# Expert weights laid out for 8 KB runs, with a stepped read in the gate and up products

## The chip, the core and the metric

The kernel runs on one core of a Trainium2 chip. The metric is the device time of one execution in microseconds (us), the median of the runs shown. Smaller is better. "PE" is TensorE's matmul side, "PEld" its weight loads, "ACT" ScalarE, "DVE" VectorE, "POOL" GpSimd, "SP" SyncE, which issues most of the DMAs.

## What is computed

One layer of a streaming encoder over 576 rows (512 prompt, 64 sample) of width 1024: an input projection, two kinds of attention, an output projection, and then a mixture of experts. The change touches the experts alone:

```
scores = sigmoid(h @ w_router)                  # top 6 of 64 experts per row, within 4 of 8 groups
g = einsum('td,edf->tef', h, w_gate)            # w_gate: 64 experts x 1024 x 256
u = einsum('td,edf->tef', h, w_up)              # w_up:   64 experts x 1024 x 256
a = silu(g) * u * comb[..., None]               # comb: the routing weight, 0 where not chosen
routed = einsum('tef,efd->td', a, w_down)       # w_down: 64 experts x 256 x 1024
shared = (silu(h @ w_sg) * (h @ w_su)) @ w_sd
x = x + g2 * (routed + shared); y = rms(x) * g_final
```

Everything is float32. An expert has 3 matrices of 1 MB (1.049 million bytes) each.

## The kernel before

The program is written engine by engine, with semaphores by hand; the order on each engine is the order of the code. It has three stages. Up to about 567 us come the projections, attention, the router and the sorting of rows to experts. From 567 to 1211 us runs the expert loop. From 1211 us the routed rows are summed and the shared expert and the last norm follow.

**Items.** The 576 x 6 = 3,456 pairs of row and expert are cut into items of at most 64 rows of one expert (`SLOT = 64`), and every expert has at least one. With the inputs used here the routing gives, expert by expert, 1 2 1 1 3 2 2 2 1 1 1 1 2 1 1 1 1 1 1 2 1 1 2 1 1 2 1 1 1 2 3 1 2 2 2 1 1 3 1 2 1 1 1 2 1 1 1 1 1 1 2 1 2 3 1 1 1 1 2 1 1 1 2 1 items, 90 in all. `START` holds the first item of each expert.

**One item.** GpSimd gathers the item's rows of `h_rows` (the normed rows, stored to memory by ACT, L1165 to L1171) into `HG[x]` (`gather`, L508), two half rows of 512 columns per row: partition 64h+s holds half h of row s. ACT copies them to `HGS` (L1186), PE transposes four 128-column blocks (`turn_in`, L917), and DVE copies the result to `HGT`, so that block k of the contraction (k from 0 to 7) is `HGT[:, k % 4, k // 4, :]`. `gate_up` (L920 to L925) makes 16 float32 products: for each k, and for n = 0 and 1, a 64-column stationary block of `HGT` against 256 moving columns, 128 of gate and 128 of up. n picks the half of the 256 expert columns and the half of the array (output partitions n*64). In the trace each float32 product is 2 records, so an item has 32 records of L924. Then follow the transposes of the next item (L917), the down products of the item before (`down`, L931, 8 records), and the transpose of this item's activations (L946). ACT does the silu (L1195), DVE the product with up (L1586), ACT copies the transposed activations to `AE` (L1198), DVE copies the down result to `YO[x]` (L1580, L1588), and GpSimd scatters it to `y_rows` (L516).

**Weights.** There are four buffers for gate and up (`GU[j]`) and four for down (`DN[j]`); expert e uses j = e mod 4. PE waits for all three loads of an expert at once, before its first item (`exp_ld[j]`, 48). SP issues the loads in one queue. `load_wide` (L333 to L335) brings gate and up, `load_down` (L337, L338) brings down. `refill(e, ...)` waits until the last gate/up product of expert e is done and then issues `load_wide(e + 4)`; it then waits until the down products in the first item of expert e are done and issues `load_down(e + 3)`. The first four experts are loaded ahead, gate and up at 502.6 us, down at 535.8 us, once all of `h_rows` is stored.

In these loads partition p takes rows k*128+p of gate and up, which is 8 runs of 1 KB in memory and 8 separate pieces of 1 KB in the buffer (gate and up alternate there), and rows f*128+p of down, which is 2 runs of 4 KB.

Of the kernel before, what the change touches and what calls it, by code (L numbers as in the profile page):

```python
# [19 lines left out]
P = 128  # L20
D = 1024
KC = D // P
# [11 lines left out]
FE = 256  # L34
# [11 lines left out]
def build(nc, x_prompt, x_sample, cache_a_k, cache_a_v, cache_b_k, cache_b_v, c_prompt, c_sample, w_ada, b_ada,  # L46
# [3 lines left out]
    with ctx:  # L50
# [5 lines left out]
        bank = [ctx.enter_context(nc.psum_tensor(f"bank{i}", [P, 512], F32)) for i in range(8)]  # L56
        top = [0]

        def take(n):
            top[0] += n  # L60
            assert top[0] <= N_ARENA, top[0]
            return top[0] - n

        def at(base, *shape, dt=F32):
            n = 1
            for s in shape:
                n *= s
            v = arena[:, base:base + n]
            if dt != F32:
                v = v.bitcast(dt)  # L70
            if len(shape) == 2:
                v = v.rearrange("p (a b) -> p a b", b=shape[1])
            elif len(shape) == 3:
                v = v.rearrange("p (a b c) -> p a b c", b=shape[1], c=shape[2])
            return v
# [3 lines left out]
        a_ring = take(3 * 4096)  # L79
        a_att = take(KC * T * 2 + KC * PAST + NT * D + PT * D)  # L80
# [26 lines left out]
        H2S = at(a_tmp, NT, D)  # L107
        SA = at(a_tmp + 2048, 2, T)

        GU = [RING[0], RING[1], RING[2], at(a_att, KC, 512)]  # L110
        DN = [at(a_att + 4096 + 2048 * i, 2, D) for i in (3, 0, 1, 2)]
        WSG, WSD = GU[0], DN[0]

        HG = [at(a_tmp + 512 * i, 512) for i in range(2)]
# [124 lines left out]
        lt_done, lt_evac, logit_done, sc_ready, h2t_done, h2_evac = map(sem, ("lt_done", "lt_evac", "logit_done", "sc_ready", "h2t_done", "h2_evac"))  # L239
# [4 lines left out]
        exp_ld = [sem(f"exp_ld{i}") for i in range(4)]  # L244
# [62 lines left out]
        def _(sp):  # L307
# [23 lines left out]
                for view, a, b in parts:  # L331
                    sp.dma_start(RING[g % 3][:, :, a:b], view).then_inc(ring_ld[g % 3], 16)
            def load_wide(e, j):  # L333
                sp.dma_start(GU[j][:, :, 0:FE], w_gate[0, bass.ds(e, 1)].rearrange("e (k p) n -> p (e k) n", p=P)).then_inc(exp_ld[j], 16)
                sp.dma_start(GU[j][:, :, FE:2 * FE], w_up[0, bass.ds(e, 1)].rearrange("e (k p) n -> p (e k) n", p=P)).then_inc(exp_ld[j], 16)  # L335

            def load_down(e, j):  # L337
                sp.dma_start(DN[j], w_down[0, bass.ds(e, 1)].rearrange("e (f p) n -> p (e f) n", p=P)).then_inc(exp_ld[j], 16)  # L338


            sp.wait_ge(wo_done, NT)
            for j in range(4):
                load_wide(j, j)
            sp.wait_ge(tr_done, 27)
            sp.wait_ge(h2_stored, 16 * NT)
            for j in range(4):
                load_down(j, j)
            sp.wait_ge(start_ready, 1)

            def refill(e, j, down):  # L350

                first = sp.value_load(START[0:1, bass.ds(e + 1, 1)], min_val=1, max_val=NI)
                sp.wait_ge(gu_done, first)
                load_wide(e + 4, j)
                if down:
                    first = sp.value_load(START[0:1, bass.ds(e, 1)], min_val=1, max_val=NI)
                    sp.wait_ge(dn_done, first + 1)
                    load_down(e + 3, (j + 3) % 4)
# [6 lines left out]
            first = sp.value_load(START[0:1, NE - 4:NE - 3], min_val=1, max_val=NI)  # L365
            sp.wait_ge(dn_done, first + 1)
            load_down(NE - 1, 3)

            first = sp.value_load(START[0:1, NE - 3:NE - 2], min_val=1, max_val=NI)
# [9 lines left out]
            for t in range(NT):  # L379
# [4 lines left out]
                r = ROWS[t]  # L384
                rows = y_rows[t * P * YK:(t * P + r) * YK, :].rearrange("(p k) d -> p k d", k=YK)
                for k, part in YB[t]:
                    sp.dma_start(part[0:r], rows[:, k:k + part.shape[1], :]).then_inc(yb_ld[t], 16)
            for t in range(NT):
                sp.wait_ge(y_ready, t + 1)
                r = ROWS[t]  # L390
# [168 lines left out]
        def _(pe):  # L559
# [92 lines left out]
            for n in range(6):  # L652
                g = G_IN + n
                pe.wait_ge(ring_ld[g % 3], ring_count(g))
                w = RING[g % 3]
# [4 lines left out]
                for t in range(NT if n % 3 == 2 else 4):  # L660
# [9 lines left out]
                    else:  # L670
                        pe.wait_ge(before, base + (3 if t < 2 else 5))
                        r = ROWS[t]
                        for k in range(KC):
                            if t < 4:
                                last = pe.matmul(bank[t][:, :], HT[:, k, t * P:t * P + P], w[:, k, :], start=(k == 0), stop=(k == KC - 1))  # L675
                            else:

                                for x in range(2):
                                    last = pe.matmul(bank[4][x * TS:x * TS + TS, 0:256], HT[:, k, TP:T], w[:, k, 256 * x:256 * x + 256],
                                                     start=(k == 0), stop=(k == KC - 1))  # L680
# [7 lines left out]
            for j in range(PT):  # L688
                for a in range(2):
                    q = 2 * NT + 2 * j + a  # L690
                    pe.wait_ge(kb_evac, q - 1)
                    b = bank[5 + 2 * (q % 2)]
# [161 lines left out]
            w = [RING[(G_OUT + n) % 3] for n in range(2)]  # L854
# [31 lines left out]
            for t in range(NT):  # L886
                if t >= 2:
                    pe.wait_ge(h2_evac, t - 1)
                r = ROWS[t]
# [8 lines left out]
            for u in range(NT * TOPK):  # L898
                t, k = divmod(u, TOPK)
# [19 lines left out]

            def gate_up(j):  # L920
                for k in range(KC):
                    w = GU[j][:, k, :].rearrange("p (g f) -> p g f", f=FE)
                    for n in range(2):
                        last = pe.matmul(bank[0][n * SLOT:n * SLOT + SLOT, 0:2 * P].rearrange("p (g f) -> p g f", f=P), HGT[:, k % 4, k // 4, :],  # L924
                                         w[:, :, n * P:n * P + P], start=(k == 0), stop=(k == KC - 1))  # L925
                last.then_inc(gu_done, 1)

            def down(j):
                for f in range(2):
                    for n in range(2):  # L930
                        last = pe.matmul(bank[3][n * SLOT:n * SLOT + SLOT, :], AE[:, f, :], DN[j][:, f, 512 * n:512 * n + 512], start=(f == 0), stop=(f == 1))  # L931
                last.then_inc(dn_done, 1)

            def item(i, j, before):

                pe.wait_ge(hgt_ready, i + 1)
                gate_up(j)
                pe.wait_ge(hg_staged, i + 2)
                pe.sem_inc(pe_mark)
                turn_in()  # L940
                pe.wait_ge(ae_ready, i + 1)
                pe.wait_ge(yo_ready, i + 1)
                down(before)
                pe.wait_ge(ac_ready, i + 1)
                pe.sem_inc(pe_mark)
                pe.transpose(bank[2][:, 0:P], AC, IDENT).then_inc(at_done, 1)  # L946
# [5 lines left out]
            with pe.Fori(0, NE // 4) as g:  # L952
                e = g * 4
# [21 lines left out]
            for t in range(NT):  # L975
                if t == 4:
                    pe.wait_ge(acc_ready, 1)
                r = ROWS[t]
# [7 lines left out]
        def _(act):  # L986
            n = [0]
# [176 lines left out]
            for t in range(NT):  # L1164
                r = ROWS[t]  # L1165
                b = 6 if t % 2 == 0 else 0
                act.wait_ge(h2t_done, t + 1)
                act.copy(H2S[0:r, t, 0:512], bank[b][0:r, :])
                act.copy(H2S[0:r, t, 512:D], bank[b + 1][0:r, :]).then_inc(h2_evac, 1)
                act.wait_ge(h2_evac, t + 1)  # L1170
                act.dma_start(h2_rows[t * P:t * P + r, :], H2S[0:r, t, :]).then_inc(h2_stored, 16)  # L1171
            for s in range(2):
# [18 lines left out]
            with act.Fori(0, pairs) as g:  # L1191
                for x in range(2):
                    i = g * 2 + x
# [494 lines left out]
```

## Time and profile before

| | |
|---|---|
| time, median of 3 runs | 1307.94 us (1305.64 to 1310.03) |
| span of the profiled execution, first to last instruction | 1303.8 us |
| the profiled execution's own time | its span is what the profile gives; the median run is 4.1 us above that span |
| PE busy | 1130.0 us, 87% |
| ACT, DVE, POOL busy | 324.9, 391.3, 306.5 us |
| DMA | 304.18 MB in 195,436 packets, mean 233 GB/s |
| the expert stage, 567 to 1211 us | PE busy 590.2 of 644 us, DMA engines busy 0.99, 342 GB/s |

Busy shares are averages over stages with different limits, so the stage is read by itself. "PEclk" is the clock that TensorE was granted (1.0 is 2.4 GHz, 0.5 is 1.2 GHz). A DMA share near or above 1 means that the 16 DMA engines had packets all the time. A wait for several loads is put down to the one that came last.

### The profile page before, as it was taken

To read this page: it belongs to the slowest core of one execution; us is meant where nothing else is said; L and a number is where in the kernel's file an instruction comes from. 1 tells how busy PE (TensorE), PEld (TensorE's weight loads), DVE (VectorE), ACT (ScalarE), POOL (GpSimd) and SP (SyncE) were. 2 spreads that over 40 slices of the span, in tenths; PEclk is the share of its full clock that TensorE was granted. 3 is DMA by queue.
4 is the path that set the end of the run, shared out by engine and by line. 5 is a ranking of instruction groups with operands and counts; after the bars stand their busy time and mean duration, and the time that the engine had idled before them with its cause. 6 is when DMAs were issued, how large, how long until landed. Compare 5 with 4: busy or idle time off the path is not lost.

```text
span 1303.8 us, 19553 instructions
## 1 busy us (share of the span) xinstructions
PE 1130.0 (87%) x6570; PEld 656.3 (50%) x6571; DVE 391.3 (30%) x936; ACT 324.9 (25%) x708; POOL 306.5 (24%) x500
## 2 busy tenths in 40 slices
PE   3899999898999897489998698899999889988960
PEld 1676676465666544354554344455554445544630
DVE  2200000284553223622222122222222212222587
ACT  2000100295663111222222222222222212222111
POOL 1000100102222000333333233333333323333123
PEclk9699999998997898689999999999999989999995
DMA  9711321213440005729899999999999999899651
GB/s 320 278 65 65 109 93 65 74 64 130 165 159 1 1 1 186 274 88 351 310 350 372 369 374 369 369 366 314 322 340 363 369 362 371 310 368 329 258 188 72
DMA packets 195436, 304.18 MB, mean 233 GB/s; under 512 B 13206, under 2 KB 146392, under 8 KB 194568
## 3 DMA queue, kind: packets, MB, share of 16 engines
q1 hardware_dynamic: 178488, 268.26, 59.6%
q0 software_dynamic: 16256, 33.08, 7.0%
q10 hardware_dynamic: 656, 2.36, 0.5%
q8 instruction: 23, 0.38, 0.1%
q14 instruction: 13, 0.11, 0.0%
HBM read 290.26 MB, written 33.82 MB: 249 GB/s over the span
## 4 chain that ended last, share of the span: by engine, by line
PE 68%; DMA 12%; DVE 7%; SPq 7%; issue 2%; ACT 2%; POOL 1%; POOLq 0%; DVEq 0%; ACTq 0%
PE bank L924 19%; DMA arena<-in_w_down 10%; PE bank L931 9%; PE bank L616 6%; PE bank L617 6%; SPq L335 4%; PE bank L675 4%; PE bank L862 4%; PE bank L917 3%; PE bank L786 2%; PE bank L601 2%; SPq L338 1%; DVE arena L1622 1%; PE bank L813 1%; PE bank L609 1%
## 5 line engine op out<-in xcount | busy, mean ns | idle before, releaser
L924 PE MATMUL bank<-arena 128*64 128x256 f32 x2880 | 348.1, 397 | 55.4 <-DMA arena<-in_w_down 42.4
L924 PEld LDWEIGHTS bank<-arena 128*64 128x64 f32 x2880 | 211.6, 142 | 166.2 <-issue 79.8
L931 PE MATMUL bank<-arena 128*64 128x512 f32 x728 | 176.3, 605 | 0.6 <-DVE arena L1580 0.6
L1586 DVE TENSOR_TENSOR arena<-arena,bank 128x128 f32<-128x128 f32 x90 | 25.9, 288 | 385.8 <-ACT arena L1195 381.2
L508 POOL DMA_INDIRECT arena<-h_rows,arena x93 | 98.2, 1056 | 82.5 <-issue 49.8
L516 POOL DMA_INDIRECT y_rows<-arena x91 | 93.2, 1024 | 86.2 <-POOL arena L513 80.6
L616 PE MATMUL bank<-arena 128*128 128x288 f32 x320 | 105.6, 412 | 2.2 <-DVE arena L1273 2.2
L617 PE MATMUL bank<-arena 128*128 128x288 f32 x320 | 105.3, 411 | 0.0
L1580 DVE COPY arena<-bank 128x512 f32<-128x512 f32 x91 | 62.9, 692 | 113.3 <-PE bank L931 113.3
L1195 ACT ACTIVATE arena<-bank 128x128 f32<-128x128 f32 x90 | 25.0, 278 | 271.5 <-PE bank L924 271.5
L1198 ACT COPY arena<-bank 128x128 f32<-128x128 f32 x90 | 23.9, 265 | 218.8 <-PE bank L946 218.8
L931 PEld LDWEIGHTS bank<-arena 128*64 128x64 f32 x728 | 44.2, 136 | 67.8 <-issue 67.0
L513 POOL COPY arena<-arena 128x1 uint32 x91 | 16.5, 181 | 259.2 <-DVE arena L1580 259.2
L616 PEld LDWEIGHTS bank<-arena 128*128 128x128 f32 x320 | 61.5, 193 | 20.3 <-DVE arena L1273 2.4
L617 PEld LDWEIGHTS bank<-arena 128*128 128x128 f32 x320 | 61.7, 193 | 17.4
L917 PE MATMUL bank<-arena 128*128 128x128 f32 x364 | 59.7, 287 | 3.0 <-ACT arena L1186 3.0
L1588 DVE COPY arena<-bank 128x512 f32<-128x512 f32 x90 | 62.3, 692 | 0.0
L1186 ACT COPY arena<-arena 128x512 f32<-128x512 f32 x92 | 57.2, 622 | 3.4 <-DMA arena<-h_rows,arena 3.4
L1195 ACT ACT_TABLE_LOAD x45 | 57.7, 1283 | 0.8
L917 PEld LDWEIGHTS bank<-arena 128*128 128x128 f32 x364 | 38.1, 140 | 37.7 <-issue 37.7
L675 PE MATMUL bank<-arena 128*128 128x512 f32 x128 | 55.9, 592 | 0.0
L862 PE MATMUL bank<-arena 128*128 128x512 f32 x128 | 55.1, 592 | 0.0
(266 smaller groups left out, 1110.1 us busy)
## 6 DMA issues: line engine op xcount, KB each, us to landing
arena<-in_w_gate SPq DMA_DIRECT2D x64, 1024.0 KB
arena<-in_w_up SPq DMA_DIRECT2D x64, 1024.0 KB
arena<-in_w_down SPq DMA_DIRECT2D x64, 1024.0 KB
arena<-in_w_ada SPq DMA_DIRECT2D x12, 2048.0 KB, 8.0
arena<-in_w_in SPq DMA_DIRECT2D x6, 2048.0 KB, 10.8
arena<-y_rows SPq DMA_DIRECT2D x2, 3072.0 KB, 14.0
arena<-in_w_out SPq DMA_DIRECT2D x2, 2048.0 KB, 8.4
arena<-y_rows SPq DMA_DIRECT2D x2, 2048.0 KB, 16.2
```

What stands on the lines that cost most here:

```text
L508: pool.indirect_dma_start(HG[x], None, h2_halves, bass.IndirectOffsetOnAxis(ap=ICUR[:, x:x + 1], axis=0), bounds_check=2 * T - 1, oob_is_e ...
L516: pool.indirect_dma_start(y_halves, bass.IndirectOffsetOnAxis(ap=ICUR[:, 2 + x:3 + x], axis=0), YO[x], None, bounds_check=2 * T * YK - 1, ...
L616: pe.matmul(bank[a][:, 0:TH], lw, src[:, k, 0:TH], start=(k == 0), stop=(k == KC - 1))
L617: last = pe.matmul(bank[b][:, 0:TH], lw, src[:, k, TH:T], start=(k == 0), stop=(k == KC - 1))
L675: last = pe.matmul(bank[t][:, :], HT[:, k, t * P:t * P + P], w[:, k, :], start=(k == 0), stop=(k == KC - 1))
L862: last = pe.matmul(bank[WOB[t][n]][:, :], OT[:, k, t * P:t * P + P], w[n][:, k, :], start=(k == 0), stop=(k == KC - 1))
L917: last = pe.transpose(bank[1][:, c * P:c * P + P], HGS[:, c * P:c * P + P], IDENT)
L924: last = pe.matmul(bank[0][n * SLOT:n * SLOT + SLOT, 0:2 * P].rearrange("p (g f) -> p g f", f=P), HGT[:, k % 4, k // 4, :], w[:, :, n * P: ...
L931: last = pe.matmul(bank[3][n * SLOT:n * SLOT + SLOT, :], AE[:, f, :], DN[j][:, f, 512 * n:512 * n + 512], start=(f == 0), stop=(f == 1))
L1195: act.activation(SI, bank[0][:, 0:P], ACT.Silu).then_inc(silu_done, 1)
L1580: dve.tensor_copy(YO[x], bank[3][:, :]).then_inc(yo_ready, 1)
L1588: dve.tensor_copy(hgt, bank[1][:, :]).then_inc(hgt_ready, 1)
```

## The change

The contraction index of the gate and up products is renumbered. Partition p now takes rows 8p to 8p+7 of gate and of up, one run of 8 KB each, and the buffer holds gate and up one behind the other, so that each lands in one piece of 8 KB. To match, block k of the activations must hold columns 8q+k (q from 0 to 127) in place of k*128+q: the ACT copies that fill `H2S` ahead of the store to `h_rows` read PSUM with a step of eight and write runs of 64. The gather, the transposes and `HGT` stay as they are.

The index of the expert's 256 columns is renumbered too. Partition p takes rows 2p and 2p+1 of down, one run of 8 KB. So half n of the gate and up products must be the columns of parity n, and the moving operand is read with a step of two elements.

The shared expert's weights keep their layout. The programs have the same instructions in the same order on every engine. What differs is the shape of the 10 ACT copies (8 x 64 in place of 512), of the 192 expert loads (128 x 2048 in place of 128 x 8 x 256 and 128 x 2 x 1024) and the step in the 16 products.

```diff
+        gu_base = [a_ring + 4096 * i for i in range(3)] + [a_att]
+        GUE = [at(b, 2, KC, FE) for b in gu_base]
+        GE = [w[:, 0, :, :] for w in GUE]
+        UE = [w[:, 1, :, :] for w in GUE]
...
             def load_wide(e, j):
-                sp.dma_start(GU[j][:, :, 0:FE], w_gate[0, bass.ds(e, 1)].rearrange("e (k p) n -> p (e k) n", p=P)).then_inc(exp_ld[j], 16)
-                sp.dma_start(GU[j][:, :, FE:2 * FE], w_up[0, bass.ds(e, 1)].rearrange("e (k p) n -> p (e k) n", p=P)).then_inc(exp_ld[j], 16)
+                sp.dma_start(GE[j], w_gate[0, bass.ds(e, 1)].rearrange("e (p k) n -> p (e k) n", k=KC)).then_inc(exp_ld[j], 16)
+                sp.dma_start(UE[j], w_up[0, bass.ds(e, 1)].rearrange("e (p k) n -> p (e k) n", k=KC)).then_inc(exp_ld[j], 16)
 
             def load_down(e, j):
-                sp.dma_start(DN[j], w_down[0, bass.ds(e, 1)].rearrange("e (f p) n -> p (e f) n", p=P)).then_inc(exp_ld[j], 16)
+                sp.dma_start(DN[j], w_down[0, bass.ds(e, 1)].rearrange("e (p f) n -> p (e f) n", f=2)).then_inc(exp_ld[j], 16)
...
             def gate_up(j):
                 for k in range(KC):
-                    w = GU[j][:, k, :].rearrange("p (g f) -> p g f", f=FE)
+                    w = GUE[j][:, :, k, :].rearrange("p g (f n) -> p g n f", n=2)
                     for n in range(2):
                         last = pe.matmul(bank[0][n * SLOT:n * SLOT + SLOT, 0:2 * P].rearrange("p (g f) -> p g f", f=P), HGT[:, k % 4, k // 4, :],
-                                         w[:, :, n * P:n * P + P], start=(k == 0), stop=(k == KC - 1))
+                                         w[:, :, n, :], start=(k == 0), stop=(k == KC - 1))
...
-                act.copy(H2S[0:r, t, 0:512], bank[b][0:r, :])
-                act.copy(H2S[0:r, t, 512:D], bank[b + 1][0:r, :]).then_inc(h2_evac, 1)
+                rows = H2S[0:r, t, :].rearrange("p (k q) -> p k q", q=P)
+                act.copy(rows[:, :, 0:64], bank[b][0:r, :].rearrange("p (q k) -> p k q", k=KC))
+                act.copy(rows[:, :, 64:P], bank[b + 1][0:r, :].rearrange("p (q k) -> p k q", k=KC)).then_inc(h2_evac, 1)
```

## Rows read from the trace of the kernel before

**Rows 1.** The page: engines' busy us, and the DMA line of 40 slices (32.6 us each).
```profile
PE 1130.0 (87%) x6570; PEld 656.3 (50%) x6571; DVE 391.3 (30%) x936; ACT 324.9 (25%) x708; POOL 306.5 (24%) x500
...
DMA  9711321213440005729899999999999999899651
```

**Rows 2.** Windows: length, busy us per engine (instructions), PEclk, DMA share, GB/s.
```profile
567.00:1211.00 644.00, 590.22 (x4050) 305.54 (x4050) 148.17 (x269) 153.07 (x314) 221.57 (x361) 0.97 0.99 342
```

**Rows 3.** Waits: who waited for whom, us in total, times, longest us.
```profile
PE bank L924 <- DMA arena<-in_w_down: 42.4, 19, 4.4
```

**Rows 4.** Timeline of PE: start us, us, line, what, count, wait before it.
```profile
567.14 6.07 PE L924 MATMUL bank<-arena 128*64 128x256 f32 x32 [1.72 <-DVE arena L1573]
...
846.52 6.32 PE L924 MATMUL bank<-arena 128*64 128x256 f32 x32 [4.41 <-DMA arena<-in_w_down]
...
901.30 3.67 PE L924 MATMUL bank<-arena 128*64 128x256 f32 x32
...
933.07 3.67 PE L924 MATMUL bank<-arena 128*64 128x256 f32 x32
...
940.31 3.67 PE L924 MATMUL bank<-arena 128*64 128x256 f32 x32 [0.86 <-issue]
...
1183.09 5.30 PE L924 MATMUL bank<-arena 128*64 128x256 f32 x32 [2.87 <-DMA arena<-in_w_down]
...
1204.92 3.67 PE L924 MATMUL bank<-arena 128*64 128x256 f32 x32
```

**Rows 5.** The chain of waits, 842 to 856 us: start us, us, what.
```profile
842.29 13.35 DMA arena<-in_w_down
855.92 3.67 PE bank L924 x32
```

**Rows 6.** Windows: the columns of rows 2.
```profile
521.00:524.00 3.00, 2.51 (x19) 2.04 (x19) 0.94 (x6) 1.23 (x1) 0.75 (x4) 1.00 1.10 348
...
30.00:36.00 6.00, 4.22 (x25) 1.73 (x25) 1.44 (x3) 0.00 (x0) 0.00 (x0) 0.73 1.05 387
...
539.00:545.00 6.00, 0.24 (x3) 0.28 (x4) 5.46 (x27) 0.00 (x0) 1.39 (x2) 0.50 1.02 416
...
1236.00:1242.00 6.00, 6.00 (x26) 4.73 (x25) 5.77 (x5) 1.15 (x1) 0.00 (x0) 1.00 1.02 436
```

**Rows 7.** The page, DMA queues and issues: packets, MB, share; issues with KB each.
```profile
q0 software_dynamic: 16256, 33.08, 7.0%
...
out<-arena POOLq DMA_DIRECT2D x2, 1024.0 KB, 7.4
out<-arena POOLq DMA_DIRECT2D x8, 256.0 KB, 7.6
...
out<-arena POOLq DMA_DIRECT2D x4, 128.0 KB, 7.5
```

**Rows 8.** Timeline of POOL and ACT, 905 to 914 us: a gather and its use.
```profile
905.65 1.05 POOL L508 DMA_INDIRECT arena<-h_rows,arena  x1 [0.86 <-issue]
...
914.27 0.62 ACT L1186 COPY arena<-arena 128x512 f32<-128x512 f32 x1
```

**Rows 9.** Timeline of ACT, DVE and PE, 530 to 536 us: the copies into H2S.
```profile
530.83 0.58 ACT L1169 COPY arena<-bank 64x512 f32<-64x512 f32 x1
...
534.61 1.26 DVE L1520 TENSOR_TENSOR arena<-arena 128x64 f32<-128x64 f32 x5
...
535.93 1.44 PE L894 MATMUL bank<-arena 128*128 128x320 f32 x2 [6.34 <-DVE arena L1520]
```

**Rows 10.** Three ACT lines by themselves: duration ns min/median/max, start, forms.
```profile
L1008 ACT ACTIVATE arena<-arena x1: 219/219/219, 4.6 to 4.6; 128x16 f32<-128x16 f32 x1
...
L1014 ACT ACTIVATE arena<-arena x1: 203/203/203, 20.5 to 20.5; 1x2 f32<-1x2 f32 x1
...
L1179 ACT ACTIVATE arena<-arena x1: 322/322/322, 562.8 to 562.8; 128x128 f32<-128x128 f32 x1
...
L1168 ACT COPY arena<-bank x5: 573/585/587, 524.4 to 530.4; 128x512 f32<-128x512 f32 x4, 64x512 f32<-64x512 f32 x1
```

## The prediction

> **What bounds the kernel now.** I read the page first: PE is busy 87% of the span and the DMA engines are full in most slices of the second half [rows 1]. That alone doesn't say which of the two sets the time, so I took the expert stage by itself [rows 2]. There the DMA engines have packets all the time (0.99) and PE is busy 590 of 644 us: both are close to being the bound. The waits then say who waits for whom: PE waits for weights 19 times, 42.4 us in all [rows 3]. The chain of waits shows the same from behind: in that stage it leaves PE for the loads and comes back to PE when down, the last of an expert's three loads, has landed, 13.35 us after its issue [rows 5]. So the stage is PE's pace where buffers are ahead, and the loads' pace where they are not.
>
> How much the loads cost in all I take from PE's timeline [rows 4]. Undisturbed items start 6.35 us apart (901.30 to 933.07 is five of them, 31.77 us; I use 6.37, since the two forms of an item differ a little). Every fourth expert, where the loop goes round, costs about 0.85 us more (the row at 940.31). 89 items at 6.37 and 15 such steps make 579.7 us. The real stretch from the first item's products (567.14) to the last's (1204.92) is 637.8 us. The loads' share is the rest, **58.1 us**: 42.4 of waits, and about 16 that follow from them. After some waits the 32 records take 5.30 or 6.32 us for 3.67 [rows 4]; the granted clock, 2.4 GHz at full, is 0.97 in the stage's mean [rows 2], so it falls to its lower level, 1.2 GHz, there. (2.4 of the 16 are the first item's own, 6.07 us, and stay.)
>
> **The change, part by part.**
>
> *Longer runs.* The same bytes are loaded. What the trace says of run length are four windows in which the DMA engines are full [rows 6]: at 521 to 524 us gate and up are under way, runs of 1 KB, and 348 GB/s move; at 30 to 36 us the input projection's weights, 2 KB, 387; at 539 to 545 us down, 4 KB, 416; at 1236 to 1242 us rows of `y_rows`, 24 KB in a piece, 436. The rate rises with the run. 8 KB lies between the last two. A packet with a fixed cost beside its bytes gives 1 KB in 47 ns per engine (348 GB/s over 16) and 4 KB in 157.5 ns, so about 10 ns fixed and 36.8 ns per KB, hence 305 ns for 8 KB: 430 GB/s. I take **424**, between 416 and 430, for all three matrices. Bounds: 387 (the runs gain only what 2 KB have) and 436.
>
> *What the stage makes of it.* An expert's 3.146 MB take 6.03 + 2.52 = 8.55 us before (348 and 416), 7.42 us at 424. The items' own rows share the engines: the software queue moves 33.08 MB, of which 4.72 are outputs stored earlier (2 x 1.05 + 8 x 0.26 + 4 x 0.13 MB) [rows 7], so 28.4 MB over 90 items, 0.315 MB or 0.79 us each. That stretches the loads by about 13%: 9.7 us per expert before, 8.4 now. An expert with one item gives PE 6.37 us of work, one with two 12.74. So before, each single-item expert lost 3.3 us of the lead that four buffers give, now 2.0. Runs of singles (experts 8 to 11, 13 to 18, 44 to 49) use the lead up.
>
> I walked the 64 experts in order with the rules of `refill`: one queue; gate/up of expert e+4 starts when the last product of expert e is done, down of e+3 when the first item of e is 5.9 us old; loads take size by rate, stretched as said; weights are usable 2 us after their last byte; a wait over 1.2 us costs 1.5 us more for the clock. The last two numbers are set by me near what the rows show (5.30 - 3.67 = 1.6 [rows 4]). With the old rates the walk gives 636.4 us for the stretch that measured 637.8, with 37.3 us of waits for 42.4, and its waits lie where the trace has them (experts 12 to 29, 46 to 50, 58 to 62). So I trust it for differences. By rate for all three matrices it gives:
> - 387: 619.2 (-17); 400: 608.5 (-28); 416: 593.2 (-43)
> - 424: **589.2 (-47)**, three waits left at experts 17 to 19 and two at 49 and 50, 6.5 us together
> - 436: 584.9 (-52); no load ever late: -58
>
> *The SP queue.* Gate and up are now 128 runs each, not 1024. The wait of 13.35 us in [rows 5] from issue to landing is queueing behind gate and up; it shrinks with the rate, and the walk has it. The number of DMAs and their order on SP, ACT and POOL stay the same.
>
> *The step of two in the moving operand.* 16 products of each item change, 3.67 us of its 6.37. No PE row of this trace reads its moving operand with a step, so the trace can't price it. The nearest rows are ACT's: L1008 reads its 16 elements with a step of eight in 219 ns, where L1014 (2 elements) and L1179 (128) give a line of 203 + 0.94 ns per further element, 216 for 16 [rows 10]. A stepped read cost at most 3 ns there. I take **0**. The upper end is reading at half rate, 3.67 us more per item; below nothing is excluded, as no fewer columns pass through the array. *What the lead costs if this fails* is the slow rival's.
>
> *The ACT copies.* 10 copies read PSUM with a step of eight. They take 585 ns each [rows 10]; at half rate they'd take about 0.47 us more each (512 elements by 0.92), 4.7 us in all, 0 by the row of L1008. PE waits there for both the copies and DVE's mask: the last copy begins at 530.83 and ends at 531.4, the mask is done at 535.9, and PE's wait ends with it [rows 9]. That covers 4.5 us; without the cover it would be up to 4.7 on the path. The store to `h_rows` goes out later by the same, but the down loads behind it have until 567. I take 0, at most 1 us.
>
> *The gathers.* They share engines with 8 KB packets now. A gather is issued at 905.65 + 1.05 and used at 914.27 [rows 8]: 7.6 us of slack. It has 16 KB per engine, 0.6 us of data. If one 8 KB packet of 0.31 us went ahead of each of 8 rows, it would need 3 us. 0.
>
> **Sum.** -47 + 0 + 0 + 0. Against the profiled execution: span 1303.8 to 1257. The median run is 4.1 us above that span, so 1307.9 - 47 = **1261 us**. A measurement of this kernel can tell about 0.3% (4 us) from no change.
>
> **Rivals.**
>
> 1. *The loads gain less.* Mixed with gathers, scatters and each other, the runs of 8 KB could move at 387 to 400. For it: the fully busy windows are of one kind of load each. Against: down's 4 KB reached 416, and the 24 KB pieces 436 with PE busy beside them. Time: 1308 - 17 to - 28, 1280 to 1291. Here belongs a ceiling of the memory side: if gate and up can rise by 3% only, with down at 416 as measured, the walk gives -7, 1301. The Trainium skill, "DMA: Bandwidth & Descriptors", section "Where 436 GB/s comes from", says that for transfers between HBM and SBUF the HBM side binds at about 358 GB/s per core. By that rule 1 KB runs are already near the ceiling and the change is worth almost nothing; the 416 and 436 of [rows 6] speak against it, and I give that ceiling 2 in 100.
>
> 2. *Slower: the stepped read makes PE the bound.* The place is L924. The walk with 424 GB/s and a longer item says from where it decides: at 6.9 us per item it is -10, at 7.0 -1, at 7.05 +4. So 0.65 us more per item, the products 18% longer (3.67 to 4.3), eat the whole gain; at half rate an item takes 10.04 us and no load matters: +270, 1578 us; at 25% longer (0.92 per item) about +25, 1333. For it: two products run side by side on the two halves of the array and read the same region, and PE has no slack in this stage. Against: only [rows 10]. The Trainium skill, "SBUF — State Buffer", section "Door 1: The DMA port swizzle", says that SBUF has lines of 16 bytes and that two hits on each line are enough for full bandwidth; a step of two float32 makes exactly two. By that rule the sum stands; no row here shows it for PE.
>
> 3. *The change doesn't do what it says*: the runs are cut into 1 KB packets all the same. Then 1308. Against: pieces of 24 KB reach 436 GB/s [rows 6], which 1 KB packets at 348 don't.
>
> **How the numbers follow.** The forecast, waits for weights mostly gone, 1249 to 1277: 0.72. Rival 1: 0.13 (0.02 of it the ceiling, still faster by over 0.3%). Rival 3 and anything within 0.3%: 0.03. Rival 2: 0.12. Faster 0.85, same 0.03, slower 0.12. The low end is the stage with no load late, 58 us less, 1250, and a little: 1249. The high end takes in the bound of 387, 1291. Left out are rival 2, rival 3 and the ceiling, some 0.17.
>
> **What would show it.** Right: the profile shows about 128 packets per load and far fewer packets in all (195,436 less 64 x 2,304 plus 64 x 384, some 73,000); full windows of gate and up near 424 GB/s; PE's wait for `in_w_down` down from 42.4 to under 10 us; 32 records of L924 still in 3.67 us and items 6.35 us apart; the stage DMA share well below 0.99; the stretch of 637.8 near 589. Wrong: 32 records take longer (rival 2); the rate stays below 400 with the waits at the same experts (rival 1); waits of ACT L1186 for the gather appear.

## The result, and the profile after

The kernel after takes 1275.2 us (median of 4 runs, 1269.7 to 1278.2). The ratio to the kernel before, run beside it, is **0.975, interval 0.972 to 0.978**: by it 32.6 us less than 1307.9 (between the two medians of this occasion, 1306.8 and 1275.2, it is 31.6). The forecast was 1261 us, 47 less. A second measurement on another occasion gave 0.975 again (0.972 to 0.979), 1276.3 us.

The page of the kernel after: span, engines' busy us, DMA share and GB/s of 40 slices (31.8 us each), and packets. They answer to [rows 1].

```profile
span 1271.1 us, 19553 instructions
...
PE 1130.2 (89%) x6570; PEld 645.8 (51%) x6571; DVE 391.2 (31%) x936; ACT 325.3 (26%) x708; POOL 306.6 (24%) x500
...
DMA  9811231222450002817789999997889999798652
GB/s 317 296 67 67 85 122 67 71 71 91 175 182 18 1 1 82 341 66 302 293 320 418 416 412 407 402 413 286 309 332 378 403 417 398 285 417 312 277 181 74
DMA packets 72556, 304.18 MB, mean 239 GB/s; under 512 B 13206, under 2 KB 15320, under 8 KB 47112
```

The same bytes travel in 72,556 packets for 195,436, so the loads are in 8 KB pieces as forecast. In the expert stage the slices that were full at 366 to 374 GB/s now reach 402 to 418, and others are below 340: there the loads are ahead and pause until buffers come free. Windows of the kernel after (length, busy us per engine with instructions, PEclk, DMA share, GB/s): the whole stage, which answers to [rows 2]; then, to set against [rows 6], gate and up ahead of the stage, a stretch with late loads, and down alone.

```profile
565.00:1179.00 614.00, 592.23 (x4050) 296.07 (x4050) 148.07 (x270) 153.18 (x314) 221.48 (x361) 0.99 0.90 359
512.00:515.00 3.00, 3.00 (x20) 1.83 (x20) 0.00 (x0) 0.00 (x0) 0.00 (x0) 0.50 1.03 434
725.00:745.00 20.00, 16.07 (x103) 8.13 (x100) 3.31 (x6) 3.41 (x7) 5.97 (x9) 0.91 1.02 419
536.00:539.00 3.00, 0.66 (x3) 0.34 (x1) 2.02 (x12) 0.00 (x0) 0.00 (x0) 0.50 1.00 418
```

The stage is now PE's: 592 of 614 us busy (590 of 644 before), with the DMA engines at 0.90 (0.99 before). While the loads are late (725 to 745 us) the mix with gathers and scatters moves 419 GB/s. The 434 is the highest of its kind: the next two windows with gate and up under way (515 to 518 and 518 to 521 us) move 410 and 421, and a second one of down (539 to 542 us) moves 429. So 8 KB runs move 410 to 434, whichever matrix it is.

Waits in the kernel after, as in [rows 3]: PE's own, and the longest of SP's.

```profile
PE bank L928 <- issue: 12.1, 16, 1.1
PE bank L928 <- DMA arena<-in_w_down: 8.0, 7, 2.5
```

```profile
SPq L338 <- PE bank L928: 411.3, 60, 32.0
```

PE waits 8.0 us for weights, 7 times, for 42.4 and 19. SP was held in the issue of loads before: the median issue of an `up` load (1,024 runs) took 3.7 us, the longest 6.0. Now (128 runs) it takes 0.38, the longest 0.65, and SP spends the time waiting for buffers to come free: 411 us, where the profile of before has 159.5 for the same wait.

The timeline of PE after, as in [rows 4]: the first item, three neighbours, the last.

```profile
565.18 6.06 PE L928 MATMUL bank<-arena 128*64 128x256 f32 x32 [1.61 <-DVE arena L1578]
...
902.15 3.84 PE L928 MATMUL bank<-arena 128*64 128x256 f32 x32
...
908.64 3.84 PE L928 MATMUL bank<-arena 128*64 128x256 f32 x32
...
915.21 3.84 PE L928 MATMUL bank<-arena 128*64 128x256 f32 x32
...
1172.64 3.84 PE L928 MATMUL bank<-arena 128*64 128x256 f32 x32
```

This is what the forecast did not have: the 32 records take **3.84 us, not 3.67**, and undisturbed items start 6.49 us apart within an expert and 6.60 from one expert to the next (medians), for 6.32 and 6.46 before. The stretch from the first item to the last is 607.5 us, for 637.8 before and 589 forecast.

The copies into `H2S`, with their step of eight in PSUM, are as long as before (median 586 ns, for 585 in [rows 10]).

```profile
L1173 ACT COPY arena<-bank x5: 572/586/587, 522.4 to 528.3; 128x512 f32<-128x512 f32 x4, 64x512 f32<-64x512 f32 x1
```

### The profile page after: what moved, and what is told of

The parts are those of the page before. It is cut to its first block, busy times and chain, and to the rows that moved or that the text cites. A ratio compares the mean times of both kernels' runs of the same rounds, so it can differ in the third digit from the quotient of the medians.

```text
span 1271.1 us, 19553 instructions
## 1 busy us (share of the span) xinstructions
PE 1130.2 (89%) x6570; PEld 645.8 (51%) x6571; DVE 391.2 (31%) x936; ACT 325.3 (26%) x708; POOL 306.6 (24%) x500
## 2 busy tenths in 40 slices
DMA packets 72556, 304.18 MB, mean 239 GB/s; under 512 B 13206, under 2 KB 15320, under 8 KB 47112
## 4 chain that ended last, share of the span: by engine, by line
PE 79%; DMA 7%; DVE 7%; issue 2%; ACT 2%; POOL 1%; SPq 0%; POOLq 0%; DVEq 0%; ACTq 0%
PE bank L928 25%; PE bank L935 12%; PE bank L620 6%; PE bank L621 6%; DMA arena<-in_w_down 5%; PE bank L679 4%; PE bank L866 4%; PE bank L921 4%; PE bank L790 2%; PE bank L950 2%; PE bank L605 2%; DVE arena L1627 1%; PE bank L613 1%; PE bank L817 1%; PE bank L766 1%
## 5 line engine op out<-in xcount | busy, mean ns | idle before, releaser
L928 PE MATMUL bank<-arena 128*64 128x256 f32 x2880 | 349.9, 394 | 23.2 <-issue 12.1
L928 PEld LDWEIGHTS bank<-arena 128*64 128x64 f32 x2880 | 202.1, 136 | 143.7 <-issue 36.7
L520 POOL DMA_INDIRECT y_rows<-arena x91 | 93.2, 1024 | 86.0 <-POOL arena L517 81.3
L935 PEld LDWEIGHTS bank<-arena 128*64 128x64 f32 x728 | 44.2, 136 | 67.9 <-issue 67.1
L1191 ACT COPY arena<-arena 128x512 f32<-128x512 f32 x92 | 57.2, 622 | 3.4 <-DMA arena<-h_rows,arena 3.4
L679 PE MATMUL bank<-arena 128*128 128x512 f32 x128 | 55.9, 592 | 0.0
```

The source lines that it names most:

```text
L520: pool.indirect_dma_start(y_halves, bass.IndirectOffsetOnAxis(ap=ICUR[:, 2 + x:3 + x], axis=0), YO[x], None, bounds_check=2 * T * YK - 1, ...
L1191: act.copy(HGS, HG[x]).then_inc(hg_staged, 1)
```

## The experiments

Two questions were open: whether the 0.17 us comes from the stepped read, and where the other missing microseconds went.

The stretch of a run, first item to last, is read from its one profiled execution, and the stage began between 558 and 570 us in these, so times and stretches need not differ by the same amount. Kernels measured on different occasions are compared by their ratios to the kernel before.

### The step alone, from both sides

**no_step**: the kernel after without the step.

```diff
-                    w = GUE[j][:, :, k, :].rearrange("p g (f n) -> p g n f", n=2)
+                    w = GUE[j][:, :, k, :]
...
-                                         w[:, :, n, :], ...
+                                         w[:, :, n * P:n * P + P], ...
```

> The kernel after, with the 8 KB loads, but the moving operand of the 16 products read in contiguous halves of 128 again. The columns of gate and up then no longer pair with the rows of down, so the routed sums are of mismatched pairs; everything else is done in full. Theory (the step of two slows the product, 3.84 us for 32 records in place of 3.67): 32 records 3.67 us, items 6.37 us apart, the stretch from first to last item about 592 us, time 1275 - 15 = about 1260. Rival (the slower product comes from the new place of gate and up, 8 KB apart in the buffer, or from the longer writes of the DMAs beside it): 3.84 us and 1275 stay.

Measured: 1265.3 us, ratio 0.971 (0.966 to 0.976). A line of this kernel's page (busy us, mean ns of one), PE's wait for weights, and one item:

```profile
L928 PE MATMUL bank<-arena 128*64 128x256 f32 x2880 | 336.7, 387 | 30.8 <-issue 14.7
```

```profile
PE bank L928 <- DMA arena<-in_w_down: 14.3, 8, 2.9
```

```profile
927.91 3.67 PE L928 MATMUL bank<-arena 128*64 128x256 f32 x32
```

The 32 records are back at 3.67 us with the same loads and the same place of the weights, so the rival (the new place of gate and up, or the longer DMA writes beside the products) falls. Busy time of the group is 336.7 us, for 349.9 in the kernel after. But the stretch is 601.8 us, 5.7 less than after and not 16: PE, quicker by itself, now waits 14.3 us for weights in place of 8.0. In time the two ratios are 0.004 apart, about 5.5 us. (The two medians, 1275.2 and 1265.3, are of different occasions.)

**step_only**: the kernel before with the step alone. As in no_step, columns of gate and up no longer pair with rows of down.

```diff
-                    w = GU[j][:, k, :].rearrange("p (g f) -> p g f", f=FE)
+                    w = GU[j][:, k, :].rearrange("p (g f n) -> p g n f", f=P, n=2)
```

> The kernel before, with its 1 KB and 4 KB loads, but the moving operand read with a step of two. The columns of gate and up then no longer pair with the rows of down. Theory: 32 records take 3.84 us, items 6.55 us apart; as this kernel waits for loads in many places, part of the 89 x 0.18 = 16 us is hidden: by the walk over the experts +7, about 1314. Rival (place or DMA writes): 3.67 us and 1307.

Measured: 1317.9 us, ratio 1.010 (1.006 to 1.015), with a stretch of 647.3 us, 9.5 longer than before. (The profiled execution is the shortest of the five, 1306.1 us; its stage began 8.8 us earlier than in the trace of before, which is why its time is hardly longer than the 1305.6 of that one. By the walk +7 us was expected.) One item of its timeline and its wait for weights:

```profile
910.13 3.84 PE L924 MATMUL bank<-arena 128*64 128x256 f32 x32
```

```profile
PE bank L924 <- DMA arena<-in_w_down: 34.9, 14, 3.6
```

3.84 us again, now with the old loads and the old place, and part of the 15 us hidden: the wait for weights falls from 42.4 to 34.9 us. The step by itself makes the kernel slower by about 1%.

### How the cost grows with the step

**step_four** and **step_three**: the kernel after with steps of four and three elements (16 and 12 bytes), over 512 and 384 neighbouring elements. The amount of work is the same, but the products use other weights than those they should.

```diff
-                    w = GUE[j][:, :, k, :].rearrange("p g (f n) -> p g n f", n=2)
+                    w = GUE[j].rearrange("p g k (f n) -> p g (k f) n", n=4)[:, :, (min(k, 6)) * (FE // 4):(min(k, 6)) * (FE // 4) + P, :]
...
-                                         w[:, :, n, :], ...
+                                         w[:, :, :, n], ...
```

```diff
-                    w = GUE[j][:, :, k, :].rearrange("p g (f n) -> p g n f", n=2)
+                    w = GUE[j].rearrange("p g k f -> p g (k f)")[:, :, min(k, 6) * FE:min(k, 6) * FE + 3 * P].rearrange("p g (f n) -> p g n f", n=3)
```

> The kernel after, with the moving operand read with a step of four elements (16 bytes), over 512 neighbouring elements of the buffer; so the products use other weights than those they should. If only the number of elements used per 16 bytes counts and two is the limit that is nearly free, this one is clearly slower than 3.84 us for 32 records: up to twice, 7.3 us, with a time of about 1275 + 89 x 3.5 = 1590. If the cost grows evenly with the step (0.17 us per doubling), 4.0 us and about 1290. If any step costs the same, 3.84 and 1275.

> The kernel after with a step of three elements (12 bytes) in the moving operand, so the products use other weights than those they should. Measured so far for 32 records: step one 3.67 us, two 3.84, four 7.42. If what counts is the number of 16-byte pieces that the operand touches (128 elements touch 32, 64, 96, 128 pieces for steps one to four), at 7.42 us for 128 pieces, step three takes 7.42 x 96 / 128 = 5.6 us, and step two lies just at the limit (3.7). Time about 1275 + 90 x 1.7 = 1430. If instead every step over two costs the double, 7.4 us and 1588.

Measured, one run each: 1587.8 and 1428.9 us (1590 and 1430 were expected). One item of each timeline, step four first:

```profile
928.00 7.42 PE L928 MATMUL bank<-arena 128*64 128x256 f32 x32
```

```profile
918.31 5.65 PE L928 MATMUL bank<-arena 128*64 128x256 f32 x32
```

For 32 records: step one 3.67, two 3.84, three 5.65, four 7.42 us. From two to four the time goes nearly with the number of 16-byte pieces touched (64, 96, 128 pieces per 128 elements; 7.42 x 96/128 = 5.57, 7.42 x 64/128 = 3.71). At two that line has come down to the contiguous read's 3.67, below which no run goes: a step of two pays 0.17 us (4.6%). That the three points lie near such a line is measured; what makes them do so is not. From two to four the number of pieces also grows just as the step does, so these runs don't tell a cost per 16-byte piece from a cost per byte spanned. A step of eight, which touches no more pieces than a step of four, would have, and was not run.

### 8 KB for gate and up alone

**gateup8k_down4k**: 8 KB runs without the step, with nothing left out. The products use contiguous halves, so down keeps rows f*128+p and runs of 4 KB.

```diff
-                sp.dma_start(DN[j], w_down[0, bass.ds(e, 1)].rearrange("e (p f) n -> p (e f) n", f=2)).then_inc(exp_ld[j], 16)
+                sp.dma_start(DN[j], w_down[0, bass.ds(e, 1)].rearrange("e (f p) n -> p (e f) n", p=P)).then_inc(exp_ld[j], 16)
```

(and the edit of no_step)

> A correct kernel with 8 KB runs for gate and up alone: contiguous halves in the products, so down keeps its rows f*128+p and runs of 4 KB. Theory: products 3.67 us; loads 5.0 us for gate and up and 2.52 for down at 418 and 416 GB/s; the walk gives 590 to 594 us for the stretch, time about 1261, so some 14 us less than the kernel after. If the 8 KB runs of down were worth much (against 4 KB), it would lie nearer 1270. Rival (place or DMA writes): 3.84 us, about 1277.

Measured: 1271.2 us, ratio 0.973 (0.968 to 0.977). That is not told apart from the kernel after (0.975), and the expected 1261 was missed: 3.67 us for the 32 records as expected, but 19.2 us of waits for weights and a stretch of 605.9 us, 12 to 16 longer than the walk over the experts said.

```profile
PE bank L928 <- DMA arena<-in_w_down: 19.2, 12, 3.3
```

Something in the walk was too kind to fast loads. I went back to it with the five stretches now measured. With weights usable 4 us after their last byte and not 2, and 418 GB/s, it gives 642 (before, measured 637.8), 650 (step_only, 647.3), 598 (no_step, 601.8), 599 (this one, 605.9) and 608 (after, 607.5). These two numbers were chosen to fit, so the agreement is no test, and 4 and 7 us stay unexplained in the two kernels that read contiguously. The traces bear out the direction: in after, PE's seven waits end 2.3 to 3.2 us after as many packets of SP's queue had landed as were asked for up to that load, in no_step its eight waits 2.8 to 4.5 us after (an estimate, as the trace doesn't say which load a packet belongs to).

### Both again, and the waits for down taken away

The next four were measured side by side. **after_again** and **no_step_again** repeat two kernels:

> The kernel after, unchanged, beside the next ones on the same chip: ratio to before 0.975, stretch from first to last item 607, waits of PE for weights 8 us.

> The kernel after with contiguous halves (columns of gate and up no longer pair with the rows of down), again, for the difference to the kernel after. Theory A (the step adds 0.17 us to each of 90 items, but 6 to 10 us of the 16 come back as longer waits for loads, which are 14 us here and 8 there): 5 to 9 us less than the kernel after. Theory B (the step costs its full 16 us of time): 14 to 17 less.

Measured: 1276.3 us, 0.975 (0.972 to 0.979), and 1267.7 us, 0.970 (0.966 to 0.973). The step costs the kernel after 8.7 us between these medians, 7.3 by the ratios and 8.2 in the stretch (610.6 and 602.4), with waits for weights of 9.2 and 13.0 us; theory A holds, theory B (14 to 17) does not. The intervals of the two ratios just overlap; the difference rests on both pairs of measurements (5.5 and 7.3 us by their ratios) and on the traces (5.7 and 8.2).

**late_down_contig** and **late_down_step**: down's loads get a semaphore of their own, and PE waits for it after the expert's first item. The first is built on gateup8k_down4k, the second on the kernel after; neither leaves anything out. The added wait is followed by a semaphore instruction of PE's, `sem_inc`.

```diff
+        dn_ld = [sem(f"dn_ld{i}") for i in range(4)]
...
-                sp.dma_start(DN[j], ...).then_inc(exp_ld[j], 16)
+                sp.dma_start(DN[j], ...).then_inc(dn_ld[j], 16)
...
-            pe.wait_ge(exp_ld[3], 48)
+            pe.wait_ge(exp_ld[3], 32)
+            pe.wait_ge(dn_ld[3], 16)
...
-                    pe.wait_ge(exp_ld[j], (g + 1) * 48)
+                    pe.wait_ge(exp_ld[j], (g + 1) * 32)
                     pe.sem_inc(pe_mark)
                     item(lo, j, (j + 3) % 4)
+                    pe.wait_ge(dn_ld[j], (g + 1) * 16)
+                    pe.sem_inc(pe_mark)
```

> Correct kernel: 8 KB runs for gate and up, 4 KB for down, contiguous halves, and the wait for down has a semaphore of its own, taken after the expert's first item (whose down products are still those of the item before) instead of ahead of it. Theory (what is left over PE's own pace is the 12 to 19 us of waits for down and the lower clock after them): the waits fall under 4 us, the stretch is 580 to 586, time some 20 us under gateup8k_down4k, about 1250, ratio 0.957. Rival (the engines simply move too few bytes, so the wait comes back at gate and up): waits and time as in gateup8k_down4k, 1270.

> Correct kernel: the kernel after, with the wait for down moved in the same way. With the waits for loads gone, nothing hides the step's 0.17 to 0.18 us per item: theory says 12 to 16 us more than late_down_contig, stretch 596 to 599, about 1264. If the step's cost is hidden elsewhere too, both have the same time.

Measured: 1262.5 us, 0.966 (0.962 to 0.969), and 1267.4 us, 0.969 (0.965 to 0.973). In both, PE's list of waits in the expert stage has no load in it any more. One stall is left in late_down_contig, ahead of expert 29, where gateup8k_down4k has its longest wait for weights (3.3 us); the profile names nothing that ended it:

```profile
PE bank L929 <- issue: 23.6, 48, 1.8
```

```profile
831.93 5.36 PE L929 MATMUL bank<-arena 128*64 128x256 f32 x32 [1.84 <-issue]
```

So, but for this place, the engines move enough bytes, and the rival falls: what was late was down, and nearly always by less than one item. The stretches are 595.3 and 605.4 us, against 605.9 and 607.5 with the early wait. But 595.3 is not the 580 to 586 expected. The timeline shows a new cost:

```profile
944.36 3.67 PE L929 MATMUL bank<-arena 128*64 128x256 f32 x32
...
950.99 3.67 PE L929 MATMUL bank<-arena 128*64 128x256 f32 x32 [0.24 <-issue]
```

An expert's first item starts 6.61 us after the item before (median of 48; here 6.63), where it was 6.46 in no_step. The step then costs 10.1 us of stretch (expected 12 to 16), as the contiguous kernel still has the stall ahead of expert 29 (with 5.36 us of products; that item and the next start 8.2 and 8.0 us after the ones before them). In time it costs 4.9 us between the medians, 4.3 by the ratios, whose intervals overlap: less than was expected, and why the time shows half of the stretch's 10 was not settled. The profiled execution of late_down_step, 1272.6 us, is one of its longer ones.

**late_down_one_less** takes away the second of the added instructions.

```diff
                     pe.wait_ge(dn_ld[j], (g + 1) * 16)
-                    pe.sem_inc(pe_mark)
```

> late_down_contig without the extra semaphore instruction behind the added wait. There, an expert's next first item started 6.62 us after the one before, against 6.46 in no_step: 0.16 us for 64 experts, 10 us. If that instruction is the cost, the pitch is 6.46 to 6.5 and the time 1253 to 1256; if the added wait itself is, nothing changes, 1262.

Measured: 1259.3 us, 0.960 (0.954 to 0.966). The pitch is 6.48 us (median of the same 48) and the stretch 592.4, with one wait for down of 1.3 us and a stall of 2.1 us ahead of expert 29. The median is 3 us lower than late_down_contig's and the ratio 0.006 lower, with overlapping intervals, where 6 to 9 us were expected; so the pitch shows where the 0.15 us went, the time by itself hardly. This kernel, complete as the two before it, has the lowest time and ratio of all, 16 us under the kernel after by the medians and 20 by the ratios.

Not run is the late wait in the kernel before, where all 19 waits for weights end with down too. By the walk, an estimate that was too kind in every kernel with fast loads, it would shorten that stretch by about 30 us, as much as the new layout did. So how much of the gain needs the 8 KB runs is open once the wait is moved.

## Why the prediction was right, and where it was off

- **What bounds the kernel: right.** The loads' pace set the stage in places, PE's elsewhere. With faster loads the DMA share fell from 0.99 to 0.90 and PE's waits for weights from 42.4 to 8.0 us ("under 10" was forecast, 6.5 by the walk), at experts 16 to 19, 29, 49 and 50; 17 to 19, 49 and 50 were forecast.
- **The rate of 8 KB runs: right.** 424 GB/s taken; 434, 410 and 421 in three windows of gate and up, 418 and 429 in two of down, 419 in the mixed, late stretch. The last is the one that counts; by the walk 418 for 424 is 3 us.
- **The step of two, taken at 0: the wrong term.** It is 0.17 us per item in both layouts, 15 us over 90 items. On the path it costs the kernel after 6 to 9 us, because the rest comes back as shorter waits for loads. ACT's 3 ns for a stepped read of 16 elements was too far a row: it was another engine's, on a short read, and did not carry over. The slow rival had the mechanism right and the size wrong: it decides from 0.65 us per item, and its full size is that of a step of four (7.42 us, 1588 us measured, 1578 given for half rate). The Trainium skill, "SBUF — State Buffer", section "Door 1: The DMA port swizzle", has two hits on a 16-byte line as enough for full bandwidth. That holds to within 4.6% here, and three and four elements per step are slower by 54% and 102%.
- **The walk over the experts: 13 us too kind.** With contiguous reading the stretch should be 589 by it, and was 602 twice. By the refitted walk 3 us of this is the rate, about 6 the 2 us of latency, which 4 fits better, and 2.4 the first item's lower clock, which the text named and then left out of the walk; the rest is open. Set against the kernel before alone, both latencies fitted within 1%: a check at one working point did not fix a constant that matters at another.
- **The clock in the walk: rough.** The walk let every longer wait cost 1.5 us more. Behind the first item the trace of before has 15 waits for weights of 1.3 to 4.4 us; 8 precede an item whose products take 5.1 to 6.3 us, and 7, up to 2.9 us long, one whose products take 3.67.
- **The sum**: of the 47 forecast, 32.6 came. By the two pairs, 6 to 9 of the missing 14 went to the step, and the rest, 5 to 9, to the walk. Both errors went the same way, so none hid the other; together they took the result to 2 us from the end of the main range, 1249 to 1277.
- **Costs at nothing**: the ACT copies (586 ns for 585) and the gathers (ACT's L1191 waits for one only ahead of the second item, 2.3 us, for 2.5 before) cost nothing, as said. The Trainium skill, "DMA: Bandwidth & Descriptors", section "Where 436 GB/s comes from", has the HBM side bind at about 358 GB/s per core. In this program that ceiling is ruled out by the 410 to 434 measured.

## What to carry to other kernels

Where both an engine and the DMA engines look full, price a change by walking the stage with both paces: here some 12% more bytes per second, with contiguous reads, shortened the stretch by 36 us (no_step), and 0.17 us per item took back 6 to 8 of a possible 15. A layout that makes transfers longer pays for it at the reader: a step of two float32 in a moving operand cost 4.6% here, a step of three 54%. Wait for a buffer where it is first read, not where its neighbours are: moving one wait by an item brought 8 to 9 us more in each layout (ratio 0.973 to 0.966, and 0.975 to 0.969), a quarter of what the whole change did.

## What the runs showed of the hardware

- Rate by run length with the DMA engines full: 348 GB/s at 1 KB, 387 at 2 KB, 416 at 4 KB [rows 6], 410 to 434 at 8 KB. Down at 8 KB or 4 KB made no difference that the times can tell (no_step 0.971 and gateup8k_down4k 0.973); the stretches are 601.8 and 602.4 with 8 KB, 605.9 with 4 KB.
- The issue of a 1 MB load on SP in this kernel: 3.7 us (median; longest 6.0) for `up` in 1,024 runs, 0.38 us in 128 runs.
- A moving operand read with a step of two, three or four float32 takes 3.84, 5.65 and 7.42 us for 32 records of 128 x 256 that take 3.67 contiguous.
- ACT reads PSUM with a step of eight float32 at the pace of a contiguous read (586 and 585 ns for 512 columns).
- One more semaphore instruction on PE behind a wait, once per expert, made the step from one expert to the next 0.14 us longer (6.61 and 6.48 us).
